# Inverse of the 64x64 triangles built in compact 32x32 blocks instead of full 64x64 blocks, in a chunked linear-recurrence scan

## What is computed

```
def wkv7_scan(S0, r, decay, kk, b, k, v, reverse, emit):
    ...
    def step(S, inp):
        r_t, w_t, kk_t, b_t, k_t, v_t = inp
        sa = jnp.einsum('bhvk,bhk->bhv', S, -kk_t)
        S = S * w_t[:, :, None, :] + sa[..., None] * b_t[:, :, None, :] + v_t[..., None] * k_t[:, :, None, :]
        y = jnp.einsum('bhvk,bhk->bhv', S, r_t) if emit else None
        return S, y
    S, ys = lax.scan(step, S0, xs, reverse=reverse)
```

## Time and profile before

| | us |
|---|---|
| median of 3 runs | 4740.95 (4729.24 to 4745.95) |
| the profiled execution, its own time | 4736.67 |
| its span, first to last instruction | 4734.9 |
| scan within it, about | 3110 to 3735 |

### The profile page before, as it was taken

The page is one execution under the profiler, slowest core; times in us unless marked ns, Lnnn a source line. Parts: engine busy times, 40 slices in busy tenths (PEclk is TensorE's granted clock), DMA queues, the critical chain, the costliest instruction groups (busy, mean ns, idle before and its releaser), DMA issues. The chain is left out here.

```text
span 4734.9 us, 81944 instructions
## 1 busy us (share of the span) xinstructions
PE 4130.6 (87%) x34438; PEld 3392.6 (72%) x34438; DVE 2731.4 (58%) x4351; ACT 1748.5 (37%) x2865; POOL 329.5 (7%) x415
## 2 busy tenths in 40 slices
PE   6999986997898998699478897978999587999997
PEld 5878864886785667488366676768888466888886
DVE  2347736884774554789345013657777644466556
ACT  2136623774463442377346111223222112222222
POOL 0000000220000000021000000023233001000000
PEclk9999996998999999799689898969898789999998
DMA  2100037994000002899300201000000031111110
GB/s 100 45 9 2 2 114 292 376 397 147 19 2 1 1 13 98 314 397 382 124 20 19 89 30 59 25 8 3 3 3 3 26 142 54 45 54 36 54 45 40
DMA packets 139161, 425.62 MB, mean 90 GB/s; under 512 B 14660, under 2 KB 50380, under 8 KB 114220
## 3 DMA queue, kind: packets, MB, share of 16 engines
q1 hardware_dynamic: 129580, 386.83, 21.2%
q0 software_dynamic: 9216, 33.56, 2.8%
HBM read 370.03 MB, written 50.33 MB: 89 GB/s over the span
## 5 line engine op out<-in xcount | busy, mean ns | idle before, releaser
L557 PE MATMUL psum<-weight_parts,h_parts 128*128 128x512 f32 (+2 forms) x2880 | 601.0, 371 | 46.0 <-DVE weight_parts L703 29.6
L557 PEld LDWEIGHTS psum<-weight_parts,h_parts 128*128 128x128 f32 x2880 | 508.2, 192 | 132.9 <-DVE weight_parts L703 30.7
L1520 DVE TENSOR_TENSOR weight_parts<-weights_raw,weight_parts 128x2048 fp32r<-128x2048 f32 x192 | 431.8, 2288 | 57.5 <-ACT weight_parts L1490 55.4
L911 ACT ACTIVATE scores<-scores,softmax_stats 128x1024 f32<-128x1024 f32 (+2 forms) x288 | 307.9, 1069 | 329.7 <-DVE softmax_stats L956 329.6
L1490 ACT ACTIVATE weight_parts<-weights_raw 128x2048 fp32r<-128x2048 f32 x192 | 360.6, 1919 | 76.8 <-DMA weights_raw<-in_moe_w_up 46.1
L1428 PE MATMUL psum<-weight_parts,picked_parts 128*128 128x512 f32 x1536 | 365.0, 398 | 16.1 <-DVE weight_parts L1520 10.8
L1901 PE MATMUL psum<-h_parts,up_parts 128*128 128x512 f32 x1536 | 355.5, 393 | 11.0 <-DVE up_parts L1976 11.0
L1917 PE MATMUL psum<-down_parts,hidden_parts 128*128 128x512 f32 x1536 | 353.5, 391 | 6.7 <-DVE down_parts L1981 6.7
L1428 PEld LDWEIGHTS psum<-weight_parts,picked_parts 128*128 128x128 f32 x1536 | 291.5, 191 | 80.1 <-issue 11.5
L703 DVE TENSOR_TENSOR weight_parts<-weights_raw,weight_parts 128x2048 fp32r<-128x2048 f32 (+2 forms) x48 | 100.7, 2098 | 426.5 <-ACT weight_parts L612 426.5
L1901 PEld LDWEIGHTS psum<-h_parts,up_parts 128*128 128x128 f32 x1536 | 291.7, 190 | 72.5 <-DVE up_parts L1976 11.8
(11 more groups left out here) (437 smaller groups left out, 7243.1 us busy)
## 6 DMA issues: line engine op xcount, KB each, us to landing
weights_raw<-in_moe_w_gate SPq DMA_DIRECT2D x64, 1024.0 KB, 14.0
weights_raw<-in_moe_w_up SPq DMA_DIRECT2D x64, 1024.0 KB, 14.1
weights_raw<-in_moe_w_down SPq DMA_DIRECT2D x64, 1024.0 KB, 13.0
w_ada<-in_w_ada SPq DMA_DIRECT2D x12, 2048.0 KB, 11.2
up_raw<-in_w_mlp_up SPq DMA_DIRECT2D x16, 1024.0 KB, 7.2
down_raw<-in_w_mlp_down SPq DMA_DIRECT2D x16, 1024.0 KB, 4.9
weights_raw<-in_even_w_in SPq DMA_DIRECT2D x10, 1024.0 KB, 5.1
weights_raw<-in_w_in SPq DMA_DIRECT2D x10, 1024.0 KB, 5.2
```

The source lines that it names most:

```text
L557: last = pe.matmul(ps[:, t, 0:width(n)], cols[:, i, KP * h + k, t * P:(t + 1) * P], part[:, n % 2, j, k, 0:width(n)], start=(h == 0 and m ...
L911: act.activation(s_b[:, i % 2, a, 0:w], s_b[:, i % 2, a, 0:w], ACT.Exp, bias=st[:, i % 4, 0, a:a + 1], scale=-1.0, accum_out=st[:, i % 4, ...
L1520: dve.tensor_tensor(part[:, n % PART_SLOTS, 1], raw[:, n % RAW_SLOTS], part[:, n % PART_SLOTS, 0].bitcast(F32), ALU.subtract).then_inc(low, 1)
```

## The change

The inverse is kept as two compact 32x32 blocks for each chunk up to the last level: `b.M` and `b.MT` are `[P, 4, 32]`, quarter r of the partitions (`QUADS`, 32 rows each) holding the diagonal block of its 32 tokens. Levels 0 to 3 use four 32x32 positions of the array with 16 moving columns. The last level multiplies the block off the diagonal from the other side, so that its result is already turned; ScalarE puts the four turned diagonal blocks (`b.MTF[Q, :, cols_of(r)]`) and the two blocks of the last level into the full turned inverse `b.MTF`, whose fourth quarter GpSimd has cleared once. The turn by TensorE and its copy go. A tile has 25 phases, `LAG` stays 6.

```
-PHASES = 26
+PHASES = 25
...
-                    for level in range(5):
-                        n = 5 * i + level
-                        pe.wait_ge(s["m_ready"], n + i + 1)
+                    for level in range(4):
+                        pe.wait_ge(s["m_ready"], 5 * i + level + 1)
                         for par, jj in HEADS:
                             h4 = slot(par, jj)
-                            for cc, C in CH:
-                                last = pe.matmul(ps[C, A, h4 * 32:(h4 + 1) * 32], b.LL[C, par, 0, jj, 0, :],
-                                                 first_blocks(b.M[C, h4], level, d), start=True, stop=True)
+                            for r, Q in QUADS:
+                                last = pe.matmul(ps[Q, A, h4 * 16:(h4 + 1) * 16], b.LL[Q, par, 0, jj, 0, cols_of(r)],
+                                                 first_blocks(b.M[Q, h4], level, d), start=True, stop=True)
...
                         for h4 in range(4):
-                            for cc, C in CH:
-                                last = pe.matmul(ps[C, B, h4 * 32:(h4 + 1) * 32], b.MT[C, h4], b.X[C, h4],
+                            for r, Q in QUADS:
+                                last = pe.matmul(ps[Q, B, h4 * 16:(h4 + 1) * 16], b.MT[Q, h4], b.X[Q, h4, 0:16],
                                                  start=True, stop=True)
                         last.then_inc(s["m_done"], 1)
                         yield
-                    pe.wait_ge(s["m_ready"], 6 * i + 6)
+                    pe.wait_ge(s["m_ready"], 5 * i + 5)
+                    for par, jj in HEADS:
+                        h4 = slot(par, jj)
+                        for cc in (0, 1):
+                            last = pe.matmul(ps[rows_of(cc, 1 - d), A, h4 * 32:(h4 + 1) * 32],
+                                             b.LL[rows_of(cc, d), par, 0, jj, 0, cols_of(1 - d)],
+                                             b.M[rows_of(cc, d), h4], start=True, stop=True)
+                    last.then_inc(s["x_done"], 1)
+                    yield
+                    pe.wait_ge(s["x_masked"], 5 * i + 5)
+                    pe.wait_ge(s["mt_ready"], 5 * i + 5)
                     for h4 in range(4):
-                        for cc, C in CH:
-                            last = pe.matmul(ps[C, A, h4 * 64:(h4 + 1) * 64], b.M[C, h4], c.ident[C, C],
-                                             start=True, stop=True)
-                    last.then_inc(s["mt_turned"], 1)
-                    yield
-                    pe.wait_ge(s["mt_copied"], i + 1)
+                        for cc in (0, 1):
+                            last = pe.matmul(ps[rows_of(cc, d), B, h4 * 32:(h4 + 1) * 32], b.X[rows_of(cc, 1 - d), h4],
+                                             b.MT[rows_of(cc, 1 - d), h4], start=True, stop=True)
+                    last.then_inc(s["m_done"], 1)
+                    yield
+                    pe.wait_ge(s["turned_spread"], 6 * i + 6)
...
@@ ScalarE
-                    for _ in range(11):
+                    for _ in range(9):
                         yield
-                    act.wait_ge(s["mt_turned"], i + 1)
-                    act.activation(flat(b.MT), ps[:, A, 0:256], ACT.Copy).then_inc(s["mt_copied"], 1)
+                    if i == 0:
+                        act.wait_ge(s["turned_cleared"], 1)
+                    act.wait_ge(s["mt_ready"], 5 * i + 5)
+                    for r, Q in QUADS:
+                        act.activation(b.MTF[Q, :, cols_of(r)], b.MT[Q], ACT.Copy).then_inc(s["turned_spread"], 1)
+                    yield
+                    act.wait_ge(s["m_done"], 5 * i + 5)
+                    for cc in (0, 1):
+                        Q = rows_of(cc, d)
+                        act.activation(b.MTF[Q, :, cols_of(1 - d)], ps[Q, B, 0:128].rearrange("p (h n) -> p h n", h=4),
+                                       ACT.Copy).then_inc(s["turned_spread"], 1)
...
@@ VectorE
-                    near = mask.neighbour_turned[:].unsqueeze(1).unsqueeze(1).to_broadcast([P, 2, 2, 64])
-                    step(dve.tensor_tensor(b.MT[:].rearrange("p (a j) n -> p a j n", a=2), b.LL[:, :, 0, :, 0, :], near,
-                                           ALU.mult))
+                    step(*[dve.tensor_tensor(b.MT[Q].rearrange("p (a j) n -> p a j n", a=2),
+                                             b.LL[Q, :, 0, :, 0, cols_of(r)],
+                                             mask.neighbour_turned[Q].unsqueeze(1).unsqueeze(1)
+                                             .to_broadcast([32, 2, 2, 32]), ALU.mult) for r, Q in QUADS])
...
-                        dve.tensor_tensor(b.X[:], ps[:, A, 0:128].rearrange("p (h n) -> p h n", h=4),
+                        dve.tensor_tensor(b.X[:, :, 0:16], ps[:, A, 0:64].rearrange("p (h n) -> p h n", h=4),
                                           wide(mask.levels[:, level]), ALU.mult).then_inc(s["x_masked"], 1)
...
-                        if level < 4:
-                            dve.wait_ge(s["m_ready"], n + i + 2)
-                            dve.transpose(flat(b.MT), flat(b.M)).then_inc(s["mt_ready"], 1)
+                        dve.wait_ge(s["m_ready"], n + 2)
+                        dve.transpose(flat(b.MT), flat(b.M)).then_inc(s["mt_ready"], 1)
                         yield
+                    dve.wait_ge(s["x_done"], 5 * i + 5)
+                    dve.tensor_copy(flat(b.X), ps[:, A, 0:128]).then_inc(s["x_masked"], 1)
```

More of the change, by code:

```diff
@@ L2222, in rwkv @@
         k.order = c.at("order_masks", 51 + 0.5 * d, [P, 2, 64])
[L2223 to L2224 removed]
+        k.neighbour_turned = c.at("neighbour_mask_turned", 52 + 0.25 * d, [P, 32])
+        k.levels = c.at("level_masks", 52.5 + 0.25 * d, [P, 4, 16])
         masks.append(k)
[L2226 removed]
+    loads = [(keep[:], dram["const_chunk_starts"][:, 0:256]), (eye[:], dram["const_block_identity"])]
     for d, k in enumerate(masks):
@@ L2458, in stream @@
                         for h4 in range(4):
-                            last = pe.matmul(ps[C, A + cc, 256 + h4 * 64:256 + (h4 + 1) * 64], b.MT[C, h4], b.Z[C, h4],
+                            last = pe.matmul(ps[C, A + cc, 256 + h4 * 64:256 + (h4 + 1) * 64], b.MTF[C, h4], b.Z[C, h4],
                                              start=True, stop=True)
@@ L2571, in stream @@
                         .then_inc(s["ends_scaled"], 1)
-                    for _ in range(14):
+                    for _ in range(13):
                         yield
@@ L2719, in scan_masks @@
 def scan_masks():
-    out = np.zeros((2, P, 416), np.float32)
+    out = np.zeros((2, P, 224), np.float32)
     a, b = np.arange(P)[:, None] % CHUNK, np.arange(CHUNK)[None, :]
@@ L2725, in scan_masks @@
     out[1, :, 0:64], out[1, :, 64:128] = -1.0 * (a > b), a >= b
-    out[0, :, 128:192] = (a % 2 == 1) & (b == a - 1)
-    out[1, :, 128:192] = (a % 2 == 0) & (b == a + 1)
-    out[0, :, 192:256] = (b % 2 == 1) & (a == b - 1)
-    out[1, :, 192:256] = (b % 2 == 0) & (a == b + 1)
-    col = np.arange(32)
-    for level in range(5):
+    a, b = np.arange(P)[:, None] % 32, np.arange(32)[None, :]
+    out[0, :, 128:160] = (b % 2 == 1) & (a == b - 1)
+    out[1, :, 128:160] = (b % 2 == 0) & (a == b + 1)
+    col = np.arange(16)
+    for level in range(4):
         n = 2 << level
@@ L2734, in scan_masks @@
             block = 2 * (col // n) + d
-            out[d, :, 256 + 32 * level:288 + 32 * level] = a // n == (block + (1 if d == 0 else -1))[None, :]
+            out[d, :, 160 + 16 * level:176 + 16 * level] = a // n == (block + (1 if d == 0 else -1))[None, :]
     return out
```

30 lines of the change are left out of this document (16 added, 14 removed).

## The result

The changed kernel takes 4745.44 us (median of 20 runs, 4734.63 to 4754.35), the kernel before 4733.93 us (median of 20, 4727.09 to 4745.95). The ratio is 1.0019, 95% interval [1.0011, 1.0027]: slower by 0.2%, that is 9 us with an interval of 5 to 13; the medians differ by 11.5. Twenty runs of each resolve less than the 0.3% that the prediction took as the limit of three runs. Forecast were 4755 us and +18.

A forecast was written before the change was run, and what follows sets the result against it. TensorE was taken to set the scan's pace, VectorE close behind, the granted clock a third limit. A 40 us shorter path and 58 us of clock loss gave +18 on 4736.67: 4755 us, range 4685 to 4835 (own range 4751 to 4790).

The forecast's parts named there:

- the path's gain at an unchanged clock: Over the scan, the dropped phase (23 us) and savings in stretches of mostly level pieces (15 us) shorten the path, say 40 us.
- The clock's term: In the scan, the share at the lower clock goes from 18% to 50%, costing 58 us (bounds 0 and 150).
- Products: TensorE's level products: 32x32 matmuls start 7 to 14 ns apart, 10 taken, 88 us less work.
- Changes of shape: TensorE in the scan: 433 more switches between array shapes at 0.1 us each, 43 us more work.
- heavy turns: Scan turns with wide products beside one or two level pieces: 0.2 us saved, 0.2 us added, so length unchanged.
- VectorE: Masks, adds and transposes shrink, the neighbour mask grows: 0.54 us less per tile and stream, 22 us over the scan.
- ScalarE: One copy becomes six: 1.8 us more per tile and stream, 7 us a round, mostly hidden; 29 us at most.
- One phase less: A tile has 25 phases instead of 26, saving one turn of 2.29 us in each of ten rounds: 23 us.
- The compact blocks: In turns of mostly level pieces, smaller VectorE operations and products ending sooner shorten the path by 15 us.
- the clock doesn't mind: Rival: small pieces affect the granted clock as the large ones did, so the kernel is faster, 4657 to 4697 us; chance 0.35.
- Everything cancels: Rival: gain and clock loss balance within 0.3% (14 us), 4740 us at a low share of 40%; chance 0.20.
- The clock stays low: Rival: wide products at 1.2 GHz can't bring the clock back, so much slower, 4847 us; chance 0.15.

The follow-up runs named there:

- wide64: The kernel before with 64 moving columns instead of 32 in all level products, same results: 4694.67 us.
- direct64_wide_26: The kernel before with the last level giving the turned block directly, 64 moving columns, and an empty phase put back (26 phases): 4682.54 us.
- direct64_wide: The kernel before with the last level giving the turned block directly, 25 phases and 64 moving columns in the level products: 4652.93 us.
- wide32_64: The changed kernel with 64 moving columns through each level product instead of 16 (32 in the last level): 4685.89 us.
- direct64_wide_shapes: 64-wide blocks, direct last level, 25 phases, 64 moving columns, plus 200 small unused 32x32 products (398 more changes of shape): 4706.95 us.
- extra_phase: The changed kernel with one empty phase put back on every engine, 26 phases to a tile: 4791.10 us.
- direct64_shapes: 64-wide blocks, direct last level, 25 phases, 32 moving columns, plus 200 small unused 32x32 products (398 more changes of shape): 4822.46 us.
- small64: The kernel before with an unused 64x64 product of 16 columns at the head of each of 400 level pieces, no change of shape: 4753.36 us.
- direct64_26: The kernel before with the last level giving the turned block directly, 32 moving columns, and an empty phase put back (26 phases): 4784.57 us.

## Why the mechanism was right and the size was not

The direction, the wide range and the mechanism held: a shorter path, paid for by a lower granted clock. The size didn't: +18 us was forecast and +11.5 measured (9 by the ratio, 5 to 13 by its interval), about half to two thirds. Of the 10 us between 4755 and 4745.44, 3 come from the base, the profiled execution's 4736.67 where 20 runs have a median of 4733.93.

The step that failed is the path's gain at an unchanged clock, put at -40 us. Closing the sum gives it: the low time rose by 215 us, worth 56 to 69 us at 0.26 to 0.32, and 11.5 less that is -44 to -57. Within it the dropped phase was put at 23 us, one turn in each of ten rounds, and the last level at nothing of its own; with the clock held they measure 31.9 and 8.8, together 41. The clock's term was 58 us and came to 56 to 69, by a low time that rose more than the 0.32 x 570 = 182 us of the prediction. The two errors are of opposite sign, and that the total came within 10 us of the forecast is partly luck. How much of the miss is in each stays open: no run shows the changed kernel, with its 16 columns, with the clock held.

With 64 columns through the level products the clock stands at 0.97 or 0.98, and the parts can be read one by one, each to about 10 us:

| step, 64 columns, clock held | kernels | us |
|---|---|---|
| direct last level, still 26 phases | wide64 to direct64_wide_26 | -8.8 |
| one phase less | direct64_wide_26 to direct64_wide | -31.9 |
| compact blocks | direct64_wide to wide32_64 | +35.2 |
| the whole change | wide64 to wide32_64 | -5.5 |

The 8.8 and the 5.5 alone are not clear of the uncertainty; the 31.9, the 35.2 and the 41 of the first two steps together are.

- *Products.* 8.7 ns apart was inside the 7 to 14, near the 10 taken.
- *Changes of shape.* 0.1 us each was about right: 0.12 and 0.13 us by two pairs of kernels, some 50 us for 433 where 43 were taken. The prediction let them cancel against the faster products in the heavy turns; alone, in direct64_wide_shapes, they cost 52 us of the kernel's time. The rule that the prediction weighed (the Trainium skill, TensorEngine Tiling (Array Packing), Key Properties: a change of mode drains TensorE) agrees with these runs in that a change costs time, and the price is about half of the full matmul of 0.22 us that the prediction tried for it.
- *VectorE.* 22 us less was forecast; it is 429.65 to 404.43, 25 us. *ScalarE.* 7 us a round more was forecast: 177.72 to 232.06 over ten rounds, 5.4 us a round, 23.2 in 60 us where 24 was named; TensorE waits 0.2 us for it in all.
- *One phase less.* The 23 us are 31.9 with the clock held, and the last level's own 8.8 us had no path term. Together 41 instead of 23. Both are measured in kernels with 64-wide blocks; in the changed kernel a phase was tried only with the clock free (extra_phase).
- *The compact blocks.* The prediction had 15 us of gain for them on the path. The changed kernel as it is, with 16 columns, was never seen with the clock held. Worked out, with 342 us of low time less at 0.26 to 0.32, it would stand at 11.5 - 89 to 11.5 - 109, that is -77 to -98 against the kernel before, where direct64_wide stands at -83.0: between 6 us slower and 15 us faster. So the 15 us are neither shown nor excluded. The same estimate against wide64 (-42.3) gives the whole path term as -35 to -56, which overlaps the -44 to -57 above.
- *The clock.* The low time rose by 215 us and not by 182. From 3280 us on the shares were nearly as said (20% to 48%); what was left out is the scan's first 172 us, which were 46% low before and 96% after. No row gives the 570 us to which the prediction applied its shares. The price of 0.32 came from counting matmuls per microsecond in stretches of different work; the runs give 0.26 to 0.32, so it was not far off. With the prediction's own price and the measured low time the clock's term is 69 us and the sum +29, farther from the measured +11.5 than the forecast was.
- *L2399 at the lower clock* and four falls in a round: right, 40 of 40 groups and 3.6 falls a round. That a heavy turn stays as long as before is not shown, since its clock is another.

Of the rivals, "the clock doesn't mind" is excluded: the low share rose from 26% to 60%, and that low time costs was shown by five pairs of kernels. "Everything cancels" has the measured time in its range (within 14 us), and the forecast's own 4751 to 4790 has not; but it gave 4740 us by a low share of 40%, and the share was 60%. "The clock stays low" is right for the first 172 us only.

So the gain of the change went here, partly by estimate: the direct last level and the dropped phase are worth 62 us in this kernel, of which part is low time saved (162 to 78 us). The compact blocks take 74 back. Their 433 changes of shape cost about 50 us in gaps (an estimate from 0.12 us each), and low time goes from 78 to 377 us, at 0.26 to 0.32 some 78 to 96 us; for the sum to be 74, the shorter products and VectorE's smaller operations must give back some 54 to 72. That changes of shape are enough for the low time is shown by direct64_shapes (78 to 380 us with only the 200 small products added; 400 of the kernel's own shape, in small64, moved it by 30). Whether the 16 columns would do the same without them was not tried.

Left open: why the same empty phase costs 44, 109 and 32 us in three kernels. The clock explains 109 against 32: (109 - 32) / 239 is 0.32 for a low microsecond. In extra_phase the 137 us of low time alone would be 36 to 44 us, which leaves 0 to 8 for the phase and not 32. Either a low microsecond costs less there, or a phase is worth less in the changed kernel; no run tells which, and so the 31.9 can't be carried over to the changed kernel with certainty. Why changes of shape and phases move the clock at all is open too; the runs show that they do.

## What to carry to other kernels

Take the granted clock of the whole stretch into the sum as a term of its own: its share from windows over all of the stretch, its beginning too, and its price by an experiment that takes low time away. If TensorE is fed small fp32 matmuls, try wider moving operands whose extra columns nobody reads: here they cost nothing up to a point (32 columns with 32x32 weights, 64 with 64x64) and gave 35 and 42 us. And split a change with two halves before judging it: the half that kept the array's shape gains 1.3% alone and 1.7% with wider products, and adding the half that changed the shape 433 times more gave all of the 1.3% back.

## What the runs showed of the hardware

- At 2.4 GHz fp32 matmuls with a 32x32 weight on four diagonal positions start 8.7 to 9 ns apart with 16 or 32 moving columns and 14 with 64. With 64x64 weights on two positions they start 29 ns apart with 32 moving columns and with 64 (wide64).
- A change between 32x32, 64x64 and 128x128 parts of the array took 0.10 and 0.15 us from start to start in the place read (3399.57 to 3400.09), and 0.13 us in the end time with the clock held (52 us for 398).
- TensorE fell to 1.2 GHz while busy by its rows: it was busy for 6.52 of the 6.8 us before 3391.0, and then low; in the changed kernel it was busy 93% of the scan and low 60% of it. (A row counts a matmul as busy over its whole length of about 0.2 us, though the next small one starts 9 ns later.) The Trainium skill (TensorE: Matmul & The Clock Gate, HAM oscillation) traces such swings in a kernel of its own to TensorE's waits for DMA between groups of matmuls; here TensorE was idle for 0.28 of those 6.8 us, so that is not what these rows show.
- An operation on 32 partitions and 128 columns takes nearly as long as one on 128 partitions: 272 against 287 ns on VectorE (L2653, L2640), 305 and 268 against 363 on ScalarE (L2550, L2555, L2513; the operations are not the same ones). The neighbour mask in four quarters costs VectorE 43.6 us in the scan where it cost 15.6 whole.
- Less work can be slower: direct64_26 leaves out the turn of the inverse by TensorE and keeps the phase, and is 46 us slower than the kernel before, with 317 us at the lower clock against 162.
